# Products that take the four PSUM banks in rotation and are evicted bank by bank, in a two-model split-precision kernel

## What is computed

```python
def first_block(x, mem, ...):                 # layer 0 = A, layer 1 = B
    mem_n = rmsnorm(mem, mem_norm)
    for layer in range(2):
        mk, mv = memory_kv(mem_n, mem_w_kv[layer], mem_k_gain[layer])
        if layer == 0:
            x = mlstm_layer(x, ..., mk, mv)    # q,k,v,o,z,mq,mz = rmsnorm(x) @ w_in; x + mix @ w_out
        else:
            k_sh, v_sh = shared_kv(x, ...)     # (rmsnorm(latent)) @ w_kv_b, 8 heads
            x = mla_layer(x, ..., k_sh, v_sh, mk, mv)
    return x

def second_block(x, mem, ...):
    u, q, k, v, gate_logits = split(rms_norm(x, g_mix) @ w_in)
    mixed = concat([pool(u), diff_attention(rope(q), rope(k), v, lam)]) * sigmoid(gate_logits)
    x = x + mixed @ w_out
    x = x + memory_cross_attention(rms_norm(x, g_cross), rms_norm(mem, g_mem), w_cq, w_ckv, w_co)
    x = x + square(relu(rms_norm(x, g_mlp) @ w_up)) @ w_down
    return rms_norm(x, g_final)
```

## Time and profile before

| | us |
|---|---|
| runs | 1695.94, 1698.38, 1700.66; median 1698.38 |
| the profiled execution | 1696.77, its span 1695.0 |
| PE busy | 1605.9 (95%), 7194 matmuls |
| DVE busy | 912.5 (54%) |
| ACT busy | 693.5 (41%) |
| POOL busy | 149.6 (9%) |
| mean granted clock of TensorE | 0.979 of full speed |

### The profile page before, as it was taken

One profiled execution on the slowest core, in us unless ns is written; L12 is line 12 of the kernel. 1 busy time (PEld: TensorE's weight loads), 2 busy tenths in 40 slices (PEclk: granted clock), 3 DMA queues, 4 the chain that ended last, 5 costly groups with the idle time before them and its releaser, 6 DMA issues.

```text
span 1695.0 us, 19322 instructions
## 1 busy us (share of the span) xinstructions
PE 1605.9 (95%) x7194; PEld 1256.8 (74%) x7194; DVE 912.5 (54%) x1856; ACT 693.5 (41%) x1587; POOL 149.6 (9%) x115
## 2 busy tenths in 40 slices
PE   7998999999999988989989999898999999999997
PEld 5767776777887776666668777678877888888885
DVE  6447474738555456556446646756454644434343
ACT  6533333323336656556334244344343432323241
POOL 3002020202110001000012000011001100000001
PEclk9999999999999999999989999999999999999998
DMA  5413121223324221112114221123232233323331
GB/s 187 143 38 95 55 63 54 84 62 114 117 74 125 77 65 49 40 39 74 61 41 133 80 62 50 50 87 118 82 112 75 88 99 100 96 91 99 100 100 50
DMA packets 90110, 141.06 MB, mean 83 GB/s; under 512 B 7457, under 2 KB 37537, under 8 KB 90017
## 3 DMA queue, kind: packets, MB, share of 16 engines
q1 hardware_dynamic: 89296, 139.02, 27.0%
q10 hardware_dynamic: 720, 0.81, 0.1%
HBM read 137.71 MB, written 2.10 MB: 82 GB/s over the span
## 4 chain that ended last, share of the span: by engine, by line
PE 76%; DVE 11%; ACT 5%; issue 3%; DMA 3%; POOL 1%; SPq 0%; POOLq 0%; ACTq 0%; DVEq 0%
PE banks L1222 16%; PE banks L1224 15%; PE banks L1223 15%; PE banks L1227 5%; PE banks L1229 5%; PE banks L1228 5%; DVE sb_arena L1886 3%; DVE sb_w_split L1886 3%; PE banks L1185 2%; ACT sb_junk L1489 2%; DVE sb_arena L1895 1%; PE banks L1413 1%; PE banks L1397 1%; PE banks L1345 1%; ACT sb_w_split L1521 1%
## 5 line engine op out<-in xcount | busy, mean ns | idle before, releaser
L1886 DVE TENSOR_TENSOR sb_w_split<-sb_raw,sb_w_split 128x512 fp32r<-128x512 f32 (+4 forms) x530 | 343.0, 689 | 398.0 <-ACT sb_w_split L1521 397.5
L1521 ACT ACTIVATE sb_w_split<-sb_raw 128x512 fp32r<-128x512 f32 (+4 forms) x530 | 288.0, 592 | 413.8 <-PE banks L1224 309.2
L1222 PE MATMUL banks<-sb_actA,sb_w_split 128*128 128x512 f32 x672 | 280.0, 417 | 7.5 <-DVE sb_arena L1886 2.9
L1224 PE MATMUL banks<-sb_actA,sb_w_split 128*128 128x512 f32 x672 | 264.9, 394 | 0.0
L1223 PE MATMUL banks<-sb_actA,sb_w_split 128*128 128x512 f32 x672 | 264.3, 393 | 0.0
L1222 PE MATMUL banks<-sb_actB,sb_w_split 128*128 128x512 f32 (+1 forms) x640 | 249.4, 390 | 10.1 <-DVE sb_arena L1886 5.0
L1224 PE MATMUL banks<-sb_actB,sb_w_split 128*128 128x512 f32 (+1 forms) x640 | 243.7, 381 | 0.0
L1223 PE MATMUL banks<-sb_actB,sb_w_split 128*128 128x512 f32 (+1 forms) x640 | 243.7, 381 | 0.0
L1227 PE MATMUL banks<-sb_w_split,sb_actA 128*128 128x512 f32 (+1 forms) x384 | 156.5, 408 | 20.9 <-DVE sb_w_split L1886 9.8
L1222 PEld LDWEIGHTS banks<-sb_actA,sb_w_split 128*128 128x128 f32 x672 | 128.2, 191 | 37.6 <-issue 11.1
L1228 PE MATMUL banks<-sb_w_split,sb_actA 128*128 128x512 f32 (+1 forms) x384 | 150.4, 392 | 0.0
(11 more groups left out here) (184 smaller groups left out, 2057.7 us busy)
## 6 DMA issues: line engine op xcount, KB each, us to landing
sb_raw<-in_a_w_in SPq DMA_DIRECT2D x66, 256.0 KB, 3.0
sb_raw<-in_w_up SPq DMA_DIRECT2D x32, 512.0 KB, 3.6
sb_raw<-in_w_down SPq DMA_DIRECT2D x32, 512.0 KB, 3.8
sb_raw<-in_w_in SPq DMA_DIRECT2D x24, 512.0 KB, 3.6
sb_raw<-in_mem_w_kv SPq DMA_DIRECT2D x16, 512.0 KB, 3.7
sb_raw<-in_w_ckv SPq DMA_DIRECT2D x16, 512.0 KB, 3.8
sb_raw<-in_a_w_in SPq DMA_DIRECT2D x15, 512.0 KB, 3.8
sb_raw<-in_a_w_out SPq DMA_DIRECT2D x12, 512.0 KB, 3.9
```

Of the source, the lines that this page charges most:

```text
L1222: pe.op.matmul(out, hi[:, cs], x.hi(k), start=i == 0, stop=False)
L1224: t = pe.op.matmul(out, lo[:, cs], x.hi(k), start=False, stop=last_i)
L1521: act.op.activation(hi[:, cs], raw[:, cs], ACT.Copy).then_inc(act.mark(m("w_hi"), 2 * n + part + 1), 1)
L1886: dve.op.tensor_tensor(out, a, b, op).then_inc(dve.mark(*mark) if mark else dve.tick(), 1)
```

## The change

`into` is no longer fixed. A product takes the next `n_out` banks of 0 to 3 behind those of the product before it (`bank_at`), so after a product of two blocks the next one begins with the other two banks. The last chunk of every product, and the first one unless `first=False`, runs bank by bank: both rows of bank 0, then both of bank 1, and so on. In the last chunk the eviction of bank j-1 is put right behind the rows of bank j, and the `soon` steps come behind all evictions. In a chunk that runs by bank, side work is let in at half.

```diff
@@ -403,9 +404,12 @@
             while step not in self.done:
                 self.force(step)
 
-    def product(self, name, before_ev=(), soon=None, into=(0, 1, 2, 3), by_bank=False):
+    def product(self, name, before_ev=(), soon=None, into=None, first=True):
         pr = PRODUCTS[name]
-        ks, i = k_tiles(name), 0
+        if into is None:
+            into = [(self.bank_at + j) % 4 for j in range(n_out(name))]
+            self.bank_at = (self.bank_at + n_out(name)) % 4
+        ks, i, n_j = k_tiles(name), 0, n_out(name)
         for c, (k0, kk) in enumerate(pr.order):
             n = len(self.chunks)
             self.chunks.append((name, c))
@@ -418,33 +422,44 @@
                 while self.n_fetch < self.n_split + RAW_SLOTS:
                     self.put(("fetch", self.n_fetch))
                     self.n_fetch += 1
-            for inner in range(kk):
-                ahead = ks[min(i + SRC_LEAD.get(pr.src, 0), len(ks) - 1)]
-                self.need(source_step(pr.src, ks[i]), source_step(pr.src, ahead))
-                banks = [(into[j], EV_EMPTIES[pr.ev]) for j in range(n_out(name))] if i == 0 else ()
-                self.put(("mm", name, i), banks)
-                for j in range(n_out(name)):
-                    for r in ((i,) if not by_bank or c < len(pr.order) - 1 else range(i, len(ks)) if not inner else ()):
+            last = c == len(pr.order) - 1
+            rows = range(i, i + kk)
+            by_bank = kk > 1 and (last or c == 0 and first)
+            for part in [rows] if by_bank else [(r,) for r in rows]:
+                for r in part:
+                    ahead = ks[min(r + SRC_LEAD.get(pr.src, 0), len(ks) - 1)]
+                    self.need(source_step(pr.src, ks[r]), source_step(pr.src, ahead))
+                    banks = [(into[j], EV_EMPTIES[pr.ev]) for j in range(n_j)] if r == 0 else ()
+                    self.put(("mm", name, r), banks)
+                for j in range(n_j):
+                    for r in part:
                         self.put(("rows", name, r, j))
-                    self.clock += row_ns(name) / n_out(name)
-                    if j < n_out(name) - 1:
-                        self.advance((i * n_out(name) + j) % 2)
-                i += 1
-                if i == len(ks):
-                    last = n_out(name) - 1
-                    place = self.place[("mm", name, 0), last]
-                    self.chunk_place.append(("full", place.bank, place.turn))
-                    self.need(*before_ev)
-                    for j in range(n_out(name)):
-                        self.put(("ev", name, j))
+                        self.clock += row_ns(name) / n_j
+                        if j < n_j - 1:
+                            self.advance((r * n_j + j) % 2)
+                    if last and part[-1] == rows[-1] and j:
+                        self.evict(name, j - 1, before_ev)
+                    if by_bank and j == n_j // 2 - 1:
+                        self.step()
+                if part[-1] == rows[-1]:
+                    if last:
+                        place = self.place[("mm", name, 0), n_j - 1]
+                        self.chunk_place.append(("full", place.bank, place.turn))
+                        self.evict(name, n_j - 1, before_ev)
                         if soon is not None:
-                            self.soon.extend(soon(j))
-                    if name[:-1] in NORM_AFTER:
-                        self.after_residual(name)
-                elif inner == kk - 1:
-                    self.counts["chunk"] += 1
-                    self.chunk_place.append(("chunk", 0, self.counts["chunk"]))
+                            for n in range(n_j):
+                                self.soon.extend(soon(n))
+                        if name[:-1] in NORM_AFTER:
+                            self.after_residual(name)
+                    else:
+                        self.counts["chunk"] += 1
+                        self.chunk_place.append(("chunk", 0, self.counts["chunk"]))
                 self.step()
+            i += kk
+
+    def evict(self, name, j, before_ev):
+        self.need(*before_ev)
+        self.put(("ev", name, j))
 
     def after_residual(self, name):
 
```

More of the change, by code:

```diff
@@ L549, in order_of_work @@
     scales(0, "a", after=[("sqp", "a", 7)], lag=0)
-    p.product("mqA", [("nsum", "a")])
+    p.product("mqA", [("nsum", "a")], first=False)
     p.ahead = SPLIT_SLOTS
@@ L600, in order_of_work @@
     p.put(("load_again",))
-    p.product("outA0")
+    p.product("outA0", first=False)
     p.put(("load_mem_again",))
@@ L673, in order_of_work @@
         p.put(("ysplit", "yB", 8 + h))
-    p.product("outB0")
+    p.product("outB0", first=False)
     p.product("outB1")
@@ L729, in order_of_work @@
     p.product("gC0", (), lambda j: [(("gateG", "gC0"),)] if j == 3 else [])
-    p.product("outC0")
+    p.product("outC0", first=False)
     p.product("outC1")
@@ L745, in order_of_work @@
         p.product(f"cvD{g}")
-    p.product("outD0")
+    p.product("outD0", first=False)
     p.product("outD1")
@@ L755, in order_of_work @@
         p.product(f"dn{b}0")
[L756 removed]
+        p.product(f"dn{b}1")
     while p.soon:
```

8 lines of the change are left out of this document (4 added, 4 removed).

## The result

The changed kernel takes 1660.6 us (median of 4 runs, 1657.19 to 1663.85) against 1699.5 us; the ratio is 0.9773, 95% interval 0.9753 to 0.9793. That is 38.9 us off, where 20.2 were summed; the forecast was 1678, and 1665 the low end of its range.

A forecast was written before the change was run, and what follows sets the result against it. The kernel was taken as TensorE's work plus some 89 us of gaps and some slow-clock stretches. Recovered 28.2 less 8.0 given back, net 20.2 off the profiled 1696.8, plus 1.6 for the median: 1678 us, range 1665 to 1690.

The forecast's parts named there:

- Term 1: Ends of two-bank products: nine waits of the next product for banks 0 and 1 go, 17.6 us recovered.
- Term 2: Three half-clock stretches behind waits at 589.61, 609.41 and 63.20 us go, 5.1 us recovered.
- Term 3: Earlier evictions elsewhere: four waits, taken as four-bank products waiting for bank 0 of the one before, go, 4.5 us recovered.
- Term 4: Waits of 3.60, 3.32 and 3.09 us where DVE reaches evictions late: only 1 us recovered, 0 to 12.
- Term 5: Side work doesn't get faster at `mzA`, 575 to 610 us, 646 to 870 us and `outB0`: 8.0 us given back.
- Edits at nothing: End of `ckvB` into `mk1`, operands asked for earlier by bank, fetch order and split places: no gain counted.
- `outB0`'s tail: Twelve matmuls that lay inside head 7's chain now lie behind it: 0.5 us given back, 0 to 2.4.
- All is kept: Rival: the gain is all kept and ends held by DVE's queue come back too, 1666 us, chance 0.12.
- Softmax rounds stay uncovered: Rival, 646 to 870 us: softmax rounds bunch up with no rows between them, slower at 1704 us, chance 0.04.
- the slow one by the clock: Rival: cycling of banks makes TensorE pause, slow stretches at ends of the 69 products, about 1737 us, chance 0.01.

The follow-up runs named there:

- the moved places: The kernel before (fixed banks, rows over all banks, evictions behind the last row) with side work let in where the changed kernel does during first and last chunks: 1680.3 us.
- the old places: The changed kernel with side work in by-bank chunks let in at the matmul counts and lane turns of the kernel before: 1673.0 us.
- the quiet end: The kernel before with no side work let in during the second half of a product's last row: 1697.6 us, ratio 0.9983.

## Why the prediction was wrong

The direction was right and given 0.89; the size was not: 38.9 us, where 20.2 were summed and 28.2 was the sum with nothing given back.

- **Term 1, two-bank ends, 17.6.** In the changed kernel all but the third banks of `mqB` and `kvB0` are free, which leaves 1.3 us: 16.3 recovered. Right in size. (`cvD0` and `cvD1` have two blocks as well; 0.18 us at the start of `outD0` is all that waited behind them.) The working said that the next product asks for the fresh banks only after 2.73 us "if that is by bank", and the run with rotation alone shows that this condition carried much of it. That the releaser named a bank didn't make it a matter of banks alone: at `outB0`, `kvB2` and `kvB3` the moved places freed the start without a rotation, while `kvB1` waited longer.
- **Term 2, the clock, 5.1.** The three stretches are gone, at 1.6 us each, but as a term it was mis-sized twice. It took three stretches of one execution as sure, where such waits bring one two times in three. And it left out all others: TensorE's busy time fell by 15.5 us, and half-clock time by 54.6 - 27.3 = 27.3 us, of which the three are 10.2. Of the rest, the stretch with the wait for POOL went with that wait. Those at `vA0`, in `outB0` and in `gC0` went or shrank while waits of 2.46, 2.38 and 2.34 us stayed there, so which wait brings a stretch differs from one execution to the next, and only the sum can be credited. The mean granted clock was 0.974 to 0.981 in all runs of the kernel before, 0.983 to 0.987 in those of the change. The Trainium skill (TensorE: Matmul & The Clock Gate, What's actually happening) puts the ramp under 1% of a typical span. By that rule the sum would have been further off, and this case's trace has more: the granted clock of 0.979 stands for (1 - 0.979) x 1695.0 = 35.6 us, 2.1% of the span, of which 8.0 lie behind 1679 us, where TensorE is busy for only 4.84 of 16.0 us; the rest is 1.6%.
- **Term 3, four-bank ends, 4.5.** Three of the four waits are gone, and 0.28 us is left at `zB0`: 4.1 recovered. The reason was half right. The moved side steps alone, with no early eviction, leave the same four as they are in the changed kernel. And the fourth, at 760.57, is a wait for the second bank of `quB3`, not for a first one. Ends of 0.3 to 0.9 us that no term priced (`ozA0`, `ckvB`, `mk1`, `qkA0` and others) gave 4.9 us more.
- **Term 4, ends held by DVE's queue, 1.** Mis-sized: `vA0` gave 1.1 and `ckD1` 2.4. The places had their part in both: with the old places `vA0` waits as before and `ckD1` loses 2.5 us, with the new places alone they lose 2.6 and 1.6. At `ckD1` all evictions still stand behind the split; the first one now stands ahead of the norm's four small operations (0.86 us), and DVE gets to the split after 0.33 us of waiting for ACT instead of 1.17. The upper end of 12 was not reached, since `vA2` stayed.
- **Term 5, given back, 8.** With the old places, side waits grow by 6.2 us, near the term. With the new ones they grow by 0.1.
- **Edits at nothing: the step that failed.** The forecast took the places of side work as what they were, but for `outB0`'s tail and one softmax round. The turn of the lanes and the half-way `step()` move 252 of the 913 side steps by one to five rows of a bank; that is worth 19.2 us alone and 12.4 on top of the rest. With the old places the change takes 1673.0, inside the range and 5 us under the forecast.
- **`outB0`'s tail, 0.5.** Right that it is small; the rows' place there changes nothing that can be measured.
- **The rivals.** None had the right reason. "All is kept" came nearest in time (1666), but `vA2` still waits. Softmax rounds stay uncovered ahead of `zB1` (2.7 us beyond the usual pace, 2.4 before), but side waits as a whole did not grow. With every product rotating, the granted clock rose from 0.979 to 0.987, so the slow one by the clock did not come. What the Trainium skill tells of it (TensorE: Matmul & The Clock Gate, A second HAM failure mode: psum-queue depth-cycling) finds no support here.

What stays open: why side work at these places makes TensorE wait so little. That the ends are freed by keeping side work off the evictions is shown by the quiet end; that its waits don't grow elsewhere in return, as they do there, is not explained. No run tried a shorter lag or other places, so it may be luck.

## What to carry to other kernels

Where one static list orders all engines, any edit that changes how often or when the planner is asked for side work is a change to the whole schedule. Cost it apart: build the kernel once with the old places and once with only the new ones, before crediting the idea. Look at both sums of waits then, at the starts of products and in side work: the quiet end took 10.6 us from the first and put 7.4 on the second. And a freed resource pays only as far as the next request: rotating banks moved a wait of 3.4 us two banks on until the order of requests was changed too.

## What the runs showed of the hardware

- A wait can cost about half as much again by the clock. At four starts of products, 17 of 26 waits of 2.2 to 3.7 us had a stretch of 3.41 or 6.83 us at half clock near their end, and none of 50 starts with 1.0 us or less had one. Such a stretch behind the three waits of the earlier trace rows lost some 1.6 us each. In the one trace where these waits were filled with matmuls whose results nobody uses, the clock there stayed at 1.00.
- The spread between runs of one kernel goes with the clock. The four runs of the change have clocks of 0.987, 0.986, 0.984 and 0.983 at 1657.2, 1658.5, 1662.7 and 1663.9 us; (0.987 - 0.983) x 1655 = 6.6 us of the 6.7 between first and last. With clocks known to 0.001, that is 5 to 8 us. The change with side work as before has 0.986 at 1666.8 and 0.982 at 1673.7 us, by the same sum 6.7 of 6.9.
